# Splitting the latent-to-key product of a decode page 512 + 512 + 128 columns instead of 3 x 384, in a two-layer MLA / RG-LRU step

## The reference, cut to what matters

```
k_nope = rmsnorm(einsum('lc,chd->lhd', c_all, w_uk), g_kn)      # 16 heads x 64 from the 256 latents
s = einsum('qhd,lhd->hql', qn, k_nope) + einsum('qhr,lr->hql', qr, kr_all)
p = softmax(where(mask, s * SOFTMAX_SCALE, -inf))
ctx = einsum('hql,lc->qhc', p, c_all)
return einsum('qhc,chd->qhd', ctx, w_uv)
```

## Time and profile before

| what | value |
|---|---|
| median of three runs | 1902.59 us (1902.4 to 1903.09) |
| the profiled execution's own time | 1902.45 us |
| its span, first to last instruction | 1900.6 us |
| TensorE matmul, busy | 1871.7 us (98%), 13021 instructions |
| TensorE weight load, busy | 1802.1 us (95%), 13021 instructions |
| VectorE, ScalarE, GpSimd, busy | 1091.6 us, 904.8 us, 805.3 us |
| three passes of a page, L1291 to L1293 | 2304 matmuls of 384 columns |

### The profile page before, as it was taken

How to read it: one execution, slowest core, us unless ns; L and a number is a source line. 1 busy time by engine, 2 the same in 40 slices (tenths; PEclk the granted TensorE clock), 3 DMA queues, 4 the chain that set the end, 5 groups by cost and what they waited for, 6 DMA issues and landing times.

```text
span 1900.6 us, 35339 instructions
## 1 busy us (share of the span) xinstructions
PE 1871.7 (98%) x13021; PEld 1802.1 (95%) x13021; DVE 1091.6 (57%) x1958; ACT 904.8 (48%) x1866; POOL 805.3 (42%) x814
## 2 busy tenths in 40 slices
PE   7999999999999999999999999999999999999998
PEld 7886679999999999999999999999999999999998
DVE  4677756565556555545645644647773564564464
ACT  4556655554555455343424333347754343443333
POOL 3340013432223224253473474385755347347335
PEclk9999999999999999999999999999999999999999
DMA  5320001211111110222333232232222233323223
GB/s 153 67 57 3 26 20 45 80 35 45 37 37 32 48 35 17 72 79 78 89 89 89 80 98 78 82 108 78 77 77 79 79 88 90 88 85 93 77 86 96
DMA packets 253094, 131.64 MB, mean 69 GB/s; under 512 B 43073, under 2 KB 250754, under 8 KB 252882
## 3 DMA queue, kind: packets, MB, share of 16 engines
q1 hardware_dynamic: 252514, 128.56, 24.2%
q10 hardware_dynamic: 444, 1.29, 0.2%
HBM read 126.21 MB, written 3.61 MB: 68 GB/s over the span
## 4 chain that ended last, share of the span: by engine, by line
PE 93%; DVE 3%; ACT 1%; DMA 1%; issue 1%; SPq 0%; POOL 0%; DVEq 0%; ACTq 0%; POOLq 0%
PE ps L208 13%; PE ps L211 13%; PE ps L209 13%; PE ps L1293 7%; PE ps L1291 7%; PE ps L1292 7%; PE ps L1930 5%; PE ps L1928 5%; PE ps L1934 5%; PE ps L1321 3%; PE ps L259 2%; PE ps L251 2%; PE ps L252 2%; PE ps L1067 2%; PE ps L1258 2%; PE ps L265 1%
## 5 line engine op out<-in xcount | busy, mean ns | idle before, releaser
L208 PE MATMUL ps<-split,whi 128*128 128x288 f32 x1840 | 541.6, 296 | 1.5 <-DVE arena L825 1.0
L209 PE MATMUL ps<-split,whi 128*128 128x288 f32 x1840 | 539.0, 294 | 0.0
L211 PE MATMUL ps<-split,wlo 128*128 128x288 f32 x1840 | 526.7, 295 | 0.0
L195 POOL TENSOR_TENSOR wlo<-raw,whi 128x1024 fp32r<-128x1024 f32 x127 | 307.1, 2420 | 378.0 <-ACT whi L172 370.6
L208 PEld LDWEIGHTS ps<-split,whi 128*128 128x128 f32 x1840 | 345.2, 188 | 3.9 <-issue 3.2
L209 PEld LDWEIGHTS ps<-split,whi 128*128 128x128 f32 x1840 | 345.2, 188 | 0.4
L211 PEld LDWEIGHTS ps<-split,wlo 128*128 128x128 f32 x1840 | 339.9, 188 | 0.0
L1291 PE MATMUL ps<-split,split 128*128 128x384 f32 x768 | 268.2, 349 | 0.0
L1541 DVE TENSOR_REDUCE ssq<-arena 128x16 f32<-128x1024 f32 x128 | 156.1, 1220 | 186.6 <-ACT arena L1403 186.6
L1403 ACT ACTIVATE arena<-ps 128x384 f32<-128x384 f32 (+1 forms) x384 | 174.5, 456 | 184.6 <-PE ps L1293 181.5
L1293 PE MATMUL ps<-split,split 128*128 128x384 f32 x768 | 257.8, 336 | 0.0
(11 more groups left out here) (345 smaller groups left out, 3580.0 us busy)
## 6 DMA issues: line engine op xcount, KB each, us to landing
raw<-in_ffn_w_up SPq DMA_DIRECT2D x96, 512.0 KB, 3.7
raw<-in_ffn_w_down SPq DMA_DIRECT2D x48, 512.0 KB, 3.9
arena<-in_cache_ckv SPq DMA_DIRECT2D x128, 128.0 KB, 2.0
raw<-in_rec_w_in SPq DMA_DIRECT2D x16, 512.0 KB, 3.9
raw<-in_attn_w_o SPq DMA_DIRECT2D x8, 512.0 KB, 4.6
raw<-in_rec_w_out SPq DMA_DIRECT2D x8, 512.0 KB, 4.4
raw<-in_attn_w_down SPq DMA_DIRECT2D x7, 512.0 KB, 7.6
raw<-in_attn_w_uq SPq DMA_DIRECT2D x48, 64.0 KB, 2.2
```

Of the source, the lines that this page charges most:

```text
L195: pool.tensor_tensor(wlo[:, t % RING, :], raw[:, t % RING, :], f32(whi[:, t % RING, :]), ALU.subtract).then_inc(w_lo, 1)
L208: pe.matmul(o, wh, a, start=first, stop=False, skip_group_check=resumed)
L209: pe.matmul(o, wh, b, start=False, stop=False, skip_group_check=resumed)
L211: mm = pe.matmul(o, wl, a, start=False, stop=last, skip_group_check=resumed)
```

## The change

The key columns become contiguous in `uk` (0 to 1023), and the query blocks lie behind them at 1024 and 1152. `page_products` has two groups instead of three. The first is 512 columns in bank 0: six matmuls. The second is 512 key columns in bank 1 and the 128 query columns in bank 2: twelve matmuls, a 512-column one and a 128-column one in turn, both of a turn with the same stationary operand. The squares become two of 512 columns, so that `kb_sq` counts two to a page; `kb_mm` still counts three, as the second group adds two. The waits for the second group's banks (`kb_sq` and `a_ev`) stand ahead of its first matmul.

```diff
 def uk_col(h):
-    return h * DN + (P if h * DN >= 768 else 0)
+    return h * DN
...
-            act.copy(uk[:, 0, k, 0:768], raw[:, t % RING, 0:768])
-            act.copy(uk[:, 0, k, 896:1152], raw[:, t % RING, 768:1024]).then_inc(w_hi, 1)
+            act.copy(uk[:, 0, k, 0:1024], raw[:, t % RING, 0:1024]).then_inc(w_hi, 1)
...
-            pool.tensor_tensor(uk[:, 1, k, 0:768], raw[:, t % RING, 0:768], f32(uk[:, 0, k, 0:768]), ALU.subtract)
-            pool.tensor_tensor(uk[:, 1, k, 896:1152], raw[:, t % RING, 768:1024], f32(uk[:, 0, k, 896:1152]),
+            pool.tensor_tensor(uk[:, 1, k, 0:512], raw[:, t % RING, 0:512], f32(uk[:, 0, k, 0:512]), ALU.subtract)
+            pool.tensor_tensor(uk[:, 1, k, 512:1024], raw[:, t % RING, 512:1024], f32(uk[:, 0, k, 512:1024]),
                                ALU.subtract).then_inc(w_lo, 1)
...
+        def query_at(par):
+            return 1024 + P * par
...
-            c0 = [0, 384, 768 if par else 896]
-            for j in range(3):
-                if later:
-                    pe.wait_ge(kb_sq, 3 * (b * PAGES + i) - 2 + j)
-                    if j == 2:
-                        pe.wait_ge(a_ev, b * PAGES + i)
-                col = slice(c0[j], c0[j] + 384)
-                for k in range(2):
-                    pe.matmul(ps[:, j, 0:384], ct(ct_hi, i)[:, k, :], uk[:, 0, k, col], start=(k == 0), stop=False)
-                    pe.matmul(ps[:, j, 0:384], ct(ct_hi, i)[:, k, :], uk[:, 1, k, col], start=False, stop=False)
-                    mm = pe.matmul(ps[:, j, 0:384], ct(ct_lo, i)[:, k, :], uk[:, 0, k, col], start=False,
-                                   stop=(k == 1))
-                mm.then_inc(kb_mm, 1)
+            if later:
+                pe.wait_ge(kb_sq, 2 * (b * PAGES + i) - 1)
+            for k in range(2):
+                for m, (left, right) in enumerate(((ct_hi, 0), (ct_hi, 1), (ct_lo, 0))):
+                    mm = pe.matmul(ps[:, 0, :], ct(left, i)[:, k, :], uk[:, right, k, 0:512], start=(k == 0 and m == 0),
+                                   stop=(k == 1 and m == 2))
+            mm.then_inc(kb_mm, 1)
+            if later:
+                pe.wait_ge(kb_sq, 2 * (b * PAGES + i))
+                pe.wait_ge(a_ev, b * PAGES + i)
+            q0 = query_at(par)
+            for k in range(2):
+                for m, (left, right) in enumerate(((ct_hi, 0), (ct_hi, 1), (ct_lo, 0))):
+                    begin, end = (k == 0 and m == 0), (k == 1 and m == 2)
+                    pe.matmul(ps[:, 1, :], ct(left, i)[:, k, :], uk[:, right, k, 512:1024], start=begin, stop=end)
+                    mm = pe.matmul(ps[:, 2, 0:HQ], ct(left, i)[:, k, :], uk[:, right, k, q0:q0 + HQ], start=begin,
+                                   stop=end)
+            mm.then_inc(kb_mm, 2)
...
-                for j in range(3):
-                    act.wait_ge(kb_mm, 3 * (b * PAGES + i) + j + 1)
+                for j in range(2):
+                    act.wait_ge(kb_mm, 3 * (b * PAGES + i) + 2 * j + 1)
                     if j == 0 and (i >= 2 or not first(b)):
                         act.wait_ge(sq_ok, b * PAGES + i - 1)
-                    if j < 2:
-                        dst, src = sqk[:, i % 2, j * 384:(j + 1) * 384], ps[:, j, 0:384]
-                    else:
-                        dst, src = sqk[:, i % 2, 768:1024], ps[:, 2, P * par:P * par + 256]
-                    act.activation(dst, src, ACT.Square).then_inc(kb_sq, 1)
+                    act.activation(sqk[:, i % 2, 512 * j:512 * j + 512], ps[:, j, :], ACT.Square).then_inc(kb_sq, 1)
...
-                act.copy(a_sb[g % 2][:, i % 4, :], ps[:, 2, q0:q0 + HQ]).then_inc(a_ev, 1)
+                act.copy(a_sb[g % 2][:, i % 4, :], ps[:, 2, 0:HQ]).then_inc(a_ev, 1)
```

More of the change, by code:

```diff
@@ L1364, in query_act @@
             act.copy(qr_s[2 * DR:3 * DR, par, :], rope)
-            c0 = 768 if par else 1152
+            c0 = query_at(par)
             act.copy(uk[:, 0, :, c0:c0 + P], f32(qabs[0][:, :, bass.ds(b, 1), :]).rearrange("p k a q -> p k (a q)"))\
@@ L1394, in seq_act @@
                     hi_act(act, b + 1, 1 - par, 0)
-                for j in range(3):
-                    act.wait_ge(kb_mm, 3 * (b * PAGES + i) + j + 1)
+                for j in range(2):
+                    act.wait_ge(kb_mm, 3 * (b * PAGES + i) + 2 * j + 1)
                     if j == 0 and (i >= 2 or not first(b)):
                         act.wait_ge(sq_ok, b * PAGES + i - 1)
-                    if j < 2:
-                        dst, src = sqk[:, i % 2, j * 384:(j + 1) * 384], ps[:, j, 0:384]
-                    else:
-                        dst, src = sqk[:, i % 2, 768:1024], ps[:, 2, P * par:P * par + 256]
-                    act.activation(dst, src, ACT.Square).then_inc(kb_sq, 1)
-                g, q0 = i // 4, 0 if par else 256
+                    act.activation(sqk[:, i % 2, 512 * j:512 * j + 512], ps[:, j, :], ACT.Square).then_inc(kb_sq, 1)
+                g = i // 4
                 if i % 4 == 0 and (i >= 8 or not first(b)):
                     act.wait_ge(g_s1, b * 4 + g - 1)
-                act.copy(a_sb[g % 2][:, i % 4, :], ps[:, 2, q0:q0 + HQ]).then_inc(a_ev, 1)
+                act.copy(a_sb[g % 2][:, i % 4, :], ps[:, 2, 0:HQ]).then_inc(a_ev, 1)
                 if i % 4 == 0 and (i or not first(b)):
@@ L1539, in seq_dve @@
                 n = b * PAGES + i
-                dve.wait_ge(kb_sq, 3 * n + 3)
+                dve.wait_ge(kb_sq, 2 * n + 2)
                 dve.tensor_reduce(ssq[:, (i // 4) % 2, (i % 4) * NH:(i % 4 + 1) * NH],
@@ L1607, in wo_first @@
                     pe.wait_ge(o_pl, 2 * DC)
-                    pe.wait_ge(kb_sq, 3 * PAGES * NB)
+                    pe.wait_ge(kb_sq, 2 * PAGES * NB)
                     pe.wait_ge(a_ev, PAGES * NB)
```

## The result

The changed kernel took 1945.97 us in the median of four runs (1943.6 to 1946.33) against 1902.57 before: a ratio of 1.0222, with a 95% interval of 1.021 to 1.0234. That is 43.4 us more where 36.1 were forecast, and 1.5 us above the range's upper end. The profiled execution took 1945.67 us with a span of 1943.9. Measured again later beside the kernel before, the same kernel took 1942.76 us in the median of five runs (1942.34 to 1943.42), against 1902.95: 1.021, interval 1.0196 to 1.0224, 39.8 us more.

The account below looks back on a forecast made before the run. TensorE's own pace was taken as the bound. The profiled 1902.45 us plus 36.6 for the pages, less 0.5 for VectorE's waits, plus 0.1 behind the last page, gave 1938.7 us, range 1931.5 to 1944.5.

Parts of the forecast that it names:

- The bound: Page stage: TensorE is busy throughout and waits for nobody but 0.4 us after the last page; only its pace counts.
- The short passes: Six 128-column passes a page: each exposes the next weight load, 0.113 us a slot (0.108 to 0.116), 0.678 us together.
- The long passes: Twelve 512-column passes a page: 0.228 us each (0.226 to 0.230), from the prompt's value product; 2.736 us together.
- The 384-column passes: A page before the change: eighteen slots of 0.1738 us, 3.128 us together.
- The rope product: L1302, 128 columns, at the page boundary: escapes the exposed load on pages other than the last, as fp32 transposes follow.
- The sum: A page costs 3.414 us against 3.128: 0.286 us more on 128 pages, 36.6 us in all.
- What stood outside the sum: The rest of the kernel outside the page stage: grows by nothing.
- No DMA and no clock changes: Whole kernel: DMA and clock stay as they were, since TensorE stays as dense as it is.
- Squares, banks, VectorE: Page stage: 512-column squares take 600 ns, banks have 0.6 to 0.75 us to spare, VectorE's waits shrink by 0.5 us.
- the hidden load: Rival: the load behind a short pass hides, slot 0.067 us, about 1903.3 us in all; chance 0.04.
- the half-pulled load: Rival: the load behind a short pass starts half-way, slot 0.09 us, 18.9 us more, about 1921 us; chance 0.03.
- Late banks: Rival: ScalarE reaches the second square late, TensorE waits ahead of the second group; at most 18 us more, 1957; chance 0.04.

Follow-up runs that it names:

- e2: The changed kernel with each short pass streaming 256 columns (the keys of two heads again, and the queries) instead of 128; 1949.47 us, ratio 1.0241.
- e8: The changed kernel with the six short passes in a row behind the second group's six long ones; 1940.94 us, ratio 1.0196.
- e9: The e8 kernel with a later page's two or three fp32 transposes moved from the page's start to between the first short passes; 1936.9 us, ratio 1.0182.
- e1: The kernel before with groups of 448, 448 and 256 columns in place of three of 384; 1905.31 us, ratio 1.0013.
- e7: The changed kernel with the short pass ahead of the long one in each pair, so a long one is last; 1942.64 us, ratio 1.0205.
- e3: The changed kernel with only the first of a page's six short passes, so the query product is incomplete; 1878.36 us in a single run.

## Why the prediction was wrong, point by point

- **The bound**: right. TensorE waits for nobody in the stage, before or after. Of 43.2 us between the two profiled executions 39.9 were lost there, and 3.3 outside it.
- **The short passes**: right in cause, and close in size. The load of 128 columns behind a 128-column pass is exposed: 0.108 us a slot, five times a page, where 0.113 was taken. e2 and e8 exclude the columns, the change of length and the change of bank as the cause. e9 changes the kind of the load behind two or three of them, and with it the place of the transposes, and gets part of the cost back. The last of the six takes 0.126 on average. Together 667 ns a page, 678 forecast.
- **The long passes**: the term of the sum that was mis-sized. 0.228 us from the prompt's value product, with 0.230 as upper bound. In the page stage they take 0.227 to 0.236, 2788 ns for twelve instead of 2736. That is 52 ns a page, the largest error, and over the stated bound of 0.230 for most of them.
- **The 384-column passes**: 3139 ns, not 3128. The first six of a page take 176, the others 173; the row used covered some of both.
- **The rope product**: misread. The prediction has L1302 escape the exposed load on all pages but the last. It does on 92 of 128, with a slot of 62 ns. On the 36 on which an fp32r load stands behind it, the slot is 110 ns, in the kernel before and in the one after. This costs the sum nothing, as it is the same in both, but the kernel before held the price of a short pass 36 times, and two places had been used.
- **The sum**: 3455 - 3139 = 316 ns a page instead of 286. The difference of 30 is 52 - 11 - 11 from the three points above, and 30 ns x 128 is 3.8 us. The stage grew by 39.9, and 36.6 less 0.5 had been summed. The 0.5 for VectorE came as forecast: the stretches between the pages' passes are 98.8 us in all before and 98.2 after. This error alone gives about 1942.5 us, inside the range.
- **What stood outside the sum**: "No DMA and no clock changes" failed in the first executions. The wait near 126 us, with the half clock behind it, put the stage 2.85 us later, and 0.5 came behind the stage. 1938.7 + 3.8 + 3.3 is 1945.8, and 1945.97 was measured. Either error alone would have stayed inside the range; both together carry the median past 1944.5. The step was wrong in assuming that a part of the kernel with small waits keeps its time from one execution to the next, and that its clock does.
- **Squares, banks, VectorE**: as worked out. The square takes 598 ns (600), the banks are free in time. The wait behind the last page is 0.6 us, 0.2 more than before, as said.
- **The rivals**: the hidden load is out (slot 0.108). So is the half-pulled load (0.09). The Trainium skill's figure of 81 ns for a 128-column matmul in such a stream, in "TensorE: Matmul & The Clock Gate", section "Back-to-back issue gap", does not hold here: every short pass behind which an fp32r load stands takes 108 ns or more. The Trainium skill's rule for a load, in the same page's section "LDWEIGHTS (loading the stationary operand)", 107 ns for 128 columns, does for the fp32r loads; behind the fp32 ones of the transposes, also of 128 columns, a short pass has 0.06 us. Late banks did not occur.
- **The signs named ahead**: the short slot, the long pass's 0.05 us and TensorE's lack of waits came as said. "The rest of the kernel by nothing" did not, and the 512-column slot is 4 ns off 0.228 on average and 8 at most, which by its own sign ("more than a few ns") is a miss.

## What to carry to other kernels

In these kernels a matmul's slot with fp32r operands is about the larger of two times: its own columns at the upper clock level plus some 8 to 25 ns, and the weight load of the matmul behind it. Here the load was 0.108 us, so a pass of 128 columns cost nearly as much as one of 256 (0.117). The rule misses the last pass of a page by up to 25 ns. When a width is to be split among matmuls with loads of their own, split it so that no piece is shorter than the load, evenly if need be: 3 x 384 beats 2 x 512 + 128 by 40 us in 128 pages, though columns and matmul counts are the same. If a short pass can't be avoided, a matmul with a short load behind it gives part of the cost back: in e9 two or three such places on nearly every page were worth 46 ns a page.

Before you give a small difference to a change, look for time outside the stage that was changed. Here 3.3 of 43.2 us came from there, and a second set of executions of the same program did not have most of them.

None of the kernels tried that computes the whole result beats the kernel before. Its only short pass, L1302, has a transpose behind it already on 92 of 128 pages; on the other 36 it pays 110 ns instead of 62, and no run tried to change that.

## What the runs showed that I had not expected

- The load that stands behind a short pass costs by its kind: the slot is 0.108 us with the latents' load (fp32r) behind it and 0.06 with that of a transpose's fp32 operand, both 128 x 128.
- Passes of the same width are some ns slower in the first third of a page than later: 176 against 173 ns for 384 columns, 231 against 228 on average for 512 in e8. A contention with the other engines' reads and writes at the page's start would fit, but no run tested it.
- The last pass of a page takes 11 to 18 ns more on average in all kernels with short passes near the end (e1, e2, e7, e8, the changed one), 4 before and none in e3. Where it is a short one, this stands almost only on the pages with a transpose behind the rope product.
- The same program took 1946 us in three of four executions, and 1942.3 to 1943.6 in six others. In the two profiles, a wait of 2.0 us at one place, with the lower clock behind it, makes nearly all of the difference, and the wait goes back to an instruction of VectorE that lasted 3.0 us instead of 0.82 beside one of GpSimd.
